# A one-core transformer kernel: its first stage gets filler products, another order of the first matmuls, and one row tile scaled on VectorE

## The reference, cut to what matters

```python
def _layer_norm(x, g, b):
    mu = jnp.mean(xf, axis=-1, keepdims=True)
    var = jnp.mean(jnp.square(xf - mu), axis=-1, keepdims=True)
    y = (xf - mu) * lax.rsqrt(var + LN_EPS)
    return (y * g + b)
...
x = _layer_norm(x, ln_emb_g, ln_emb_b)
proj = x @ w_in[l]
q_a, k_a, v_a, f_a, q_r, f_r, i_r, g_r = jnp.split(proj, SPLIT_POINTS, axis=-1)
```

## Time and profile before

| | |
|---|---|
| median of 3 runs | 1553.56 us (1553.02 to 1554.49) |
| the profiled execution, its own time | 1553.23 us |
| its span in the trace | 1551.4 us |
| TensorE busy | 1500.2 us, 97% |
| VectorE / ScalarE / GpSimd busy | 1030.1 / 690.8 / 423.6 us |

### The profile page before, as it was taken

How to read it: one execution, slowest core, us unless ns; L and a number is a source line. 1 busy time by engine, 2 the same in 40 slices (tenths; PEclk the granted TensorE clock), 3 DMA queues, 4 the chain that set the end, 5 groups by cost and what they waited for, 6 DMA issues and landing times. The chain is left out here.

```text
span 1551.4 us, 20959 instructions
## 1 busy us (share of the span) xinstructions
PE 1500.2 (97%) x8416; PEld 1278.5 (82%) x8416; DVE 1030.1 (66%) x1555; ACT 690.8 (45%) x1025; POOL 423.6 (27%) x363
## 2 busy tenths in 40 slices
PE   6999998998999999999999999998999999999997
PEld 5778886787888888888988877776878999999886
DVE  7676456759678865768652654448855899995335
ACT  6644346755533344323533344443446544543232
POOL 0024315631611210000170022214432466650002
PEclk9999999999999999999999999999999999999999
DMA  8342112363344432675433422314462122224211
GB/s 312 109 150 95 63 55 96 129 221 121 114 150 176 163 109 108 218 276 212 148 109 118 133 96 95 126 50 161 153 227 109 52 107 106 101 101 161 90 73 55
DMA packets 50987, 203.61 MB, mean 131 GB/s; under 512 B 18528, under 2 KB 18784, under 8 KB 32138
## 3 DMA queue, kind: packets, MB, share of 16 engines
q1 hardware_dynamic: 37346, 172.04, 30.9%
q0 software_dynamic: 8576, 28.29, 5.0%
q10 hardware_dynamic: 4968, 1.94, 0.5%
HBM read 181.24 MB, written 21.00 MB: 130 GB/s over the span
## 5 line engine op out<-in xcount | busy, mean ns | idle before, releaser
L587 PE MATMUL ps<-xl,whi 128*128 128x512 f32 (+1 forms) x1136 | 393.2, 346 | 0.0
L1889 DVE TENSOR_TENSOR wlo<-raw,whi 128x2048 fp32r<-128x2048 f32 x89 | 217.0, 2438 | 156.3 <-ACT whi L1236 156.1
L1236 ACT ACTIVATE whi<-raw 128x512 fp32r<-128x512 f32 (+1 forms) x191 | 232.4, 1223 | 130.3 <-PE ps L588 83.8
L586 PE MATMUL ps<-xh,whi 128*128 128x256 f32 (+1 forms) x768 | 263.0, 342 | 6.2 <-DVE xl L1933 6.2
L588 PE MATMUL ps<-xh,wlo 128*128 128x256 f32 (+1 forms) x768 | 257.0, 335 | 0.0
L587 PEld LDWEIGHTS ps<-xl,whi 128*128 128x128 f32 x1136 | 216.4, 190 | 24.3
L586 PEld LDWEIGHTS ps<-xh,whi 128*128 128x128 f32 x768 | 146.9, 191 | 30.7 <-issue 18.1
L588 PEld LDWEIGHTS ps<-xh,wlo 128*128 128x128 f32 x768 | 146.8, 191 | 14.8
L586 PE MATMUL ps<-xhr,whi 128*128 128x512 f32 (+1 forms) x368 | 136.8, 372 | 2.4 <-DVE xl L1933 2.4
L588 PE MATMUL ps<-xhr,wlo 128*128 128x512 f32 (+1 forms) x368 | 136.4, 371 | 0.0
L2327 DVE SCALAR_TENSOR_TENSOR xr<-ps,pc,xr 128x511 f32<-128x511 f32 x88 | 65.3, 747 | 37.1 <-ACT xr L1236 35.6
(11 more groups left out here) (467 smaller groups left out, 3615.4 us busy)
## 6 DMA issues: line engine op xcount, KB each, us to landing
raw<-in_w_in SPq DMA_DIRECT2D x35, 1024.0 KB, 5.0
raw<-in_ffn_w SPq DMA_DIRECT2D x33, 1024.0 KB, 4.8
raw<-in_ada SPq DMA_DIRECT2D x24, 1024.0 KB, 4.8
raw<-in_w_up SPq DMA_DIRECT2D x22, 1024.0 KB, 4.8
raw<-in_w_down SPq DMA_DIRECT2D x11, 1024.0 KB, 4.8
xd<-X POOLq DMA_DIRECT2D x8, 512.0 KB, 5.5
td<-vr POOLq DMA_DIRECT2D x16, 256.0 KB, 3.0
raw<-td SPq DMA_DIRECT2D x4, 1024.0 KB, 4.7
```

Of the source, the lines that this page charges most:

```text
L586: pe.e.matmul(o, lh, rh, start=start, stop=False)
L587: pe.e.matmul(o, lh, rl, start=False, stop=False)
L1236: m = ac.e.activation(dst, src, func, **more)
L1889: up(ve.e.tensor_tensor(lo, raw[conv_at[j] % 3][:, :], hi.bitcast(F32), ALU.subtract), "wlo")
```

## The change

TensorE first issues 38 products of a 128 x 128 matrix of ones with itself (`onesf`, plain float32), before the transposes of row tiles 0 and 1, and 36 more behind them. They write to a bank that is overwritten later, and nobody reads them. Then `main_parts_first` takes the place of `two_pieces`: for c = 0 and each weight piece it issues the 16 high x high products of both its row blocks, then the 16 with the low parts of x, then the 16 with the low parts of the weights. The transposes of tile 2 stand behind the first weight piece, those of tile 3 behind the high x high products of the second. Both c = 0 blocks of the second weight piece now stand ahead of the first sine product; the second sine product still stands behind (1, 0). ScalarE no longer scales row tile 1 (VectorE does), it converts both weight pieces only after the channels of tiles 0 and 1, and piece 1 ahead of the scaling of tiles 2 and 3. VectorE makes the low parts of tile 1 ahead of the low part of weight piece 0.

```diff
--- before.py
+++ after.py
@@ -703,21 +703,62 @@
                 pe.wait_ge(sig["ln_x"], t + 1)
                 channels(t)
 
-            def beside_qr(c, i):
-                if c == 0 and i < 2:
-                    emb_rows(2 + i)
-                if c == 0 and i == 2:
-                    pe.wait_ge(sig["mlp_in"], 64)
-                    sine(0, 64, w1[:, :], zt)
-                if c == 1 and i == 0:
-                    pe.wait_ge(sig["sn"], 1)
-                    sine(1, P, w2[:, :], h1)
+            def ones(n):
+                for _ in range(n):
+                    pe.e.matmul(fills.banks[3][:, 0:P], onesf[:, :], onesf[:, :], start=True, stop=True)
+
+            def main_parts_first():
+
+                bs = [take(("qr", i), "qr", i + 1, "dense") for i in range(4)]
+                o = slice(0, 256)
+                for p in range(2):
+                    h, l = parts_of(J_QR + p)
+                    pe.wait_ge(sig["whi"], conv_no(J_QR + p))
+                    pe.wait_ge(sig["ch_hi"], 4)
+                    for m in range(2):
+                        for k in range(8):
+                            a = k * 256 + P * m
+                            pe.e.matmul(bs[2 * p + m][:, o], h[:, a:a + P], half_tokens(xh1, k, 0), start=(k == 0), stop=False)
+                    if p:
+                        emb_rows(3)
+                    pe.wait_ge(sig["ch_lo"], 4)
+                    for m in range(2):
+                        for k in range(8):
+                            a = k * 256 + P * m
+                            pe.e.matmul(bs[2 * p + m][:, o], h[:, a:a + P], half_tokens(xl1, k, 0), start=False, stop=False)
+                    pe.wait_ge(sig["wlo"], conv_no(J_QR + p))
+                    for m in range(2):
+                        for k in range(8):
+                            a = k * 256 + P * m
+                            d = pe.e.matmul(bs[2 * p + m][:, o], l[:, a:a + P], half_tokens(xh1, k, 0), start=False, stop=(k == 7))
+                        done(d, (("qr", 2 * p + m), "half"))
+                    if p == 0:
+                        emb_rows(2)
+                pe.wait_ge(sig["mlp_in"], 64)
+                sine(0, 64, w1[:, :], zt)
+                r = slice(256, 512)
+                for i in range(4):
+                    h, l = weights(J_QR + i // 2)
+                    pe.wait_ge(sig["ch_lo"], 8)
+                    for k in range(8):
+                        a = k * 256 + P * (i % 2)
+                        d = mm3(bs[i][:, r], h[:, a:a + P], l[:, a:a + P], half_tokens(xh1, k, 1), half_tokens(xl1, k, 1),
+                                k == 0, k == 7)
+                    done(d, ("qr", i))
+                    if i % 2:
+                        used(J_QR + i // 2)
+                    if i == 0:
+                        pe.wait_ge(sig["sn"], 1)
+                        sine(1, P, w2[:, :], h1)
 
             use[0] = "first"
+            pe.wait_ge(sig["cst"], 1)
+            ones(38)
             pe.wait_ge(sig["consts"], 32)
             for t in range(2):
                 emb_rows(t)
-            two_pieces(J_QR, [("qr", i) for i in range(4)], ("qr", "qr"), (1, 2, 3, 4), xh1, xl1, 8, beside_qr, "dense")
+            ones(36)
+            main_parts_first()
             use[0] = "all"
 
             def rows1(j0, name, slot0):
@@ -1318,18 +1359,17 @@
 
             ac.wait_ge(sig["cst"], 3)
             act(ss_b, eps[:, 1:2], ACT.Sqrt)
-            for t in range(2):
-                root(0, t)
-                normal(0, t)
+            root(0, 0)
+            normal(0, 0)
+            root(0, 1)
             ac.wait_ge(sig["consts"], 32)
             channels(0)
-            high(0)
             channels(1)
+            high(1)
             root(0, 2)
             root(0, 3)
             normal(0, 2)
             normal(0, 3)
-            high(1)
             channels(2)
             channels(3)
             ac.wait_ge(sig["sn_v"], 7)
@@ -1972,11 +2012,15 @@
             inverse(0, 0)
             emb_stats(1)
             inverse(0, 1)
+            _, mv1, rs1 = ln_cols(0, 1)
+            ve.wait_ge(sig["ln_nm"], 2)
+            ve.wait_ge(sig["ln_x"], 1)
+            up(ve.e.tensor_scalar(X[:, 1, :], X[:, 1, :], rs1, mv1[:, 1:2], ALU.mult, ALU.add), "ln_x")
             scaled_channels(0)
             scaled_channels(1)
             low_channels(0)
+            low_channels(1)
             low_parts(0)
-            low_channels(1)
             emb_stats(2)
             emb_stats(3)
             inverse(0, 2)
```

## The result

The changed kernel takes 1557.76 us (median of 13 runs, 1555.46 to 1560.41), the kernel before 1554.00 (13 runs, 1552.05 to 1555.86). The ratio is 1.0018, 95% interval 1.0011 to 1.0026, which is +2.8 us (1.7 to 4.0) on 1554.0: slower, just inside the 0.2% that I called the edge. The two medians themselves lie 3.8 us apart, within that interval. A second measurement of the same kernel gave 1.0016 (1.0007 to 1.0026).

What follows compares the result with a forecast made beforehand. TensorE, busy 97% of 1551.4 us, was taken as the bound. Start 3.1 us later, low clock giving back 2.2 to 2.3, sine wait adding 2.2 less 0.25: +3.0 us, forecast 1556.5 us, range 1552.6 to 1558.9.

Steps and rivals of the forecast that it cites:

- the price of a gap: TensorE's 2.2 us idle before the second sine product would not lower the clock, as around an earlier 2.59 us wait.
- first transpose T: Start of TensorE's first transposes, held back 3.7 us by the first fill: 12.0 us instead of 8.31.
- first real product S: Start of TensorE's first real product, after the second fill: 21.7 us instead of 18.56.
- idle before the second sine product: TensorE waits 2.2 us for ScalarE's sine, with only one block standing between the two sine products.
- S to f_r: Time from the first real product to the start of f_r, 27.2 us plus the 2.2 us sine wait: 29.4.
- f_r: Start of f_r on TensorE, the mark for the sum: 51.1 us instead of 48.14, +3.0 us.
- rival (a): Clock rises later under the fillers or falls between fills; another 4.83 us low adds 2.4 us, 1558.9; chance 0.14.
- gives back 2.2 to 2.3: First real products on TensorE run at the upper clock at once, saving 2.2 to 2.3 us.
- that cover: Tile 2 scaled about 5.0 us after the first real product, wanted at 5.9; anything beyond 0.9 us is added.
- (b): Light fillers, one record per product of ones: f_r at 45.5, -2.6 us, 1550.9 us; chance 0.11.
- (c): No wait for the sine, nor for f_r's weights: +0.8 us, 1554.3 us; chance 0.08.
- (d): Products of ones never raise the clock, real products slow for 4.83 us again: 1574 us; chance 0.03.

Runs made afterwards that it cites:

- shorter fills: The changed kernel with fills of 21 and 23 products of ones instead of 38 and 36: ratio to the kernel before 0.9986 (0.9976 to 0.9996).
- short fills alone: The kernel before with only fills of 21 and 32 products of ones put in, its order unchanged: ratio 1.0000 (0.9991 to 1.0009).
- the last experiment: The changed kernel with fills of 21 and 23 products and the first sine product moved behind the transposes of tile 3: ratio to before 0.9972 (0.9960 to 0.9983).
- no fills: The changed kernel without its 74 products of ones, all else as changed: ratio to the kernel before 1.0008 (0.9999 to 1.0017).
- first sine product earlier: The changed kernel, long fills kept, with the first sine product moved up by 32 products: ratio to the kernel before 0.9999 (0.9989 to 1.0008).
- new order alone: The changed kernel without any fill and with the first sine product behind the transposes of tile 3: ratio to the kernel before 0.9985 (0.9974 to 0.9995).

## Why the prediction was right

Forecast +3.0 us, measured +2.8 (1.7 to 4.0). The mechanism forecast, the start held back by the fillers and a new wait for the sine, is what the profiles show; one step of it failed, the price of a gap. The first profile came near 51.1 partly by luck: its start was 0.5 us early, and a drop of the clock that the forecast had excluded cost 1.5. The second profile, without a drop of the clock in this stage, lets each step be read:

| step | forecast | changed kernel, two profiles | |
|---|---|---|---|
| records per product of ones | 2 | 2 | right |
| us a record, upper clock | 0.1115 | 0.11 | right |
| first transpose T | 12.0 | 11.46, 12.03 | right |
| first real product S | 21.7 | 21.17, 21.73 | right |
| idle before the second sine product | 2.2 | 2.00, 2.00 | right |
| S to f_r | 29.4 | 30.82, 29.35 | right without the drop |
| f_r | 51.1 | 51.99, 51.08 | right without the drop |

**The fills hold the start back.** Shown: with 30 fillers fewer S goes from 21.17 to 16.32 at the same clock and order.

**The wait before the second sine product.** Shown: moving the first one up takes it from 2.00 to 0.19 us, and 0.19% (3 us) from the time. The intervals 0.9989 to 1.0008 and 1.0011 to 1.0026 do not meet; that of the second measurement, 1.0007 to 1.0026, just overlaps the first. The same move took 0.14% off with short fills and 0.23% with none. Against the second profile of the changed kernel, which has no drop, the time from the start to f_r falls from 29.35 to 27.55 us, the 1.8 us of the wait and no more. The rest of the 3 us may be the clock drop that comes in some runs, or noise. What share of runs has the drop stays open: one of four profiles is too few.

**The price of a gap was the wrong step.** The prediction said "Such a gap does not cost the clock" on the strength of one gap of 2.59 us that did not cost it. In the changed kernel's profile a gap of 2.00 us did, for 1.5 us (f_r 30.82 behind S instead of 29.35). It is rival (a)'s kind of loss at another place. If it comes in one run of four, as in these profiles, it adds 0.4 us to the forecast's mean, an estimate; the true share is open. Nor was the one gap a safe sample. All ten profiles of this case have a wait of 2.5 to 2.8 us at that place, and in five of them the clock fell there; of the two profiles of the changed kernel, in one. Two of them, the shorter fills and then the short fills alone:

```profile
268.53 0.77 PE L912 MATMUL ps<-kz,row 128*128 128x128 f32 x2 [2.68 <-DMA kz<-ncd]
```

```profile
270.21 0.46 PE L878 MATMUL ps<-kz,row 128*128 128x128 f32 x2 [2.76 <-DMA kz<-ncd]
```

The first pair of records takes 0.77 us, at the lower clock, the second, behind a slightly longer wait, 0.46.

**The low clock "gives back 2.2 to 2.3" fits here, under a condition that I had not weighed.** No run has the changed order with so late a start at the low clock, so this term is not measured by itself; what fits is the sum, 29.35 us from the start to f_r for 29.4. In the old order the same clock gave back nothing (48.03 against 48.14), because tile 2 and piece 1 stood next in line. In the changed kernel the start is so late that both are ready; with S at 16.3 tile 2 takes back 0.7 us. The prediction named that cover but priced it only for its own S.

**Rivals.** (a), a late rise of the clock: the rise came 3.9 us (first profile) and 5.0 us (second) after the first filler, on both sides of the 4.83 taken. Over all seven profiles with fillers it came 3.5 to 5.8 us after the first, inside the 3.5 to 6.5 of the forecast. No fall between the fills shows. (b), light fillers: refuted by 148 extra records. (c), no sine wait: refuted here, and made true by an edit. (d), ones never raise the clock: refuted. What the change loses is thus the length of the fills and the place of one product; what it has that is good, the order of ScalarE's and VectorE's work and the warm clock, comes to 0.28% in the last experiment. How that divides is not shown: no run parts TensorE's new order from ScalarE's and VectorE's, or has the scaling of tile 1 on VectorE by itself.

**Where the profiles differ behind this stage.** The two spans of the changed kernel, 1556.1 and 1556.7, do not differ by f_r's 0.9 us, since each has drops of its own further on. A stretch of both, first the changed kernel's first profile, then its second, shows such a place:

```profile
1059.00:1112.00 53.00, 45.12 (x229) 36.19 (x228) 49.03 (x64) 18.34 (x27) 28.26 (x20) 1.00 0.35 116
```

```profile
1059.00:1112.00 53.00, 45.46 (x205) 36.28 (x205) 47.41 (x60) 17.50 (x26) 26.68 (x19) 0.90 0.35 118
```

That makes two spans a poor measure for an edit of 3 us. The start of the next stage is a better one for what happens before it, yet it too comes from one profile, and the ratios over all runs decide what an edit is worth.

## What to carry to other kernels

A filler on an in-order engine has to end before the first real input is ready: size it from the trace, in the records that it really makes (two for a plain float32 product), at both clocks, and rather too short (with 21 and 23 products TensorE idled 0.16 and 0.63 us before the transposes and the clock stayed up). Before paying for a warm clock, look at what the next products wait for; where other engines are only just in time, a faster start can buy nothing until their order is changed too, as the short fills in the old order did. And when blocks are regrouped, count what still stands between the two ends of every chain that crosses to another engine and back: here one block less made a wait of 2 us.

## What the runs showed of the hardware

- Behind a gap of 2.0 us on TensorE the granted clock fell to 0.50 in one profile and stayed at 1.00 in three; at the wait of 2.5 to 2.8 us near 270 us it fell in five profiles of ten (the changed kernel's first, no fills, shorter fills, first sine product earlier, new order alone) and stayed up in the other five, the kernel before among them. The drop at 42.5 us cost 1.5 us, and the same kernel had it in one profile and not in the other; the 13 runs of the changed kernel spread over 5 us.
- The time from the first product to the upper clock varied as well: 3.9 and 5.0 us of fillers in the two profiles of the changed kernel and 3.5 to 5.8 in all seven with fillers, 3.2 us of real products without fills, 4.83 before, and over 6 us (16.92 to about 23.1) in the run with the new order alone.
- In that last run the clock was up ahead of the real products, with nothing but the 16 transposes (8.48 to 12.14 us) behind it, and down again when they began, 4.78 us of idleness later. The stretches from the end of the transposes to the start, and the slow one behind it, show it:

```profile
14.00:16.30 2.30, 0.00 (x0) 0.00 (x0) 1.96 (x4) 2.30 (x3) 0.00 (x0) 0.99 1.02 426
16.40:23.00 6.60, 6.08 (x28) 6.08 (x29) 5.87 (x12) 3.50 (x5) 0.00 (x0) 0.50 1.03 320
```

  The 0.99 could be a default where nothing is recorded, as it is in the profile of before until 23.39; here the value changes within the stretch, so I take it as a record, but it is a single case: the kernel before and the run without fills have the same 16 transposes and show no such change. The Trainium skill, "TensorE: Matmul & The Clock Gate", Part 4, says that transposes do not count as activity; this row speaks against it, and the prediction's "the 16 slow ones agree" was too quick.
